# Six conditioning groups placed later in the weight stream of a two-block transformer, with the memory rows and the bias tables loading later

## The reference, cut to what matters

```python
cond = jax.nn.silu(c)
for layer in range(DEPTH):
    mod = cond @ ada_w[layer] + ada_b[layer]
    sh1, sc1, g1, sh2, sc2, g2 = jnp.split(mod, 6, axis=-1)
    h = modulate(rmsnorm(x, norm_g[layer, 0]), sh1, sc1)
    if layer % 2 == 0:
        mixed = ssd_na_mixer(h, ab_w_in[j], ...)      # h @ w_in, two branches, y @ w_out
    x = x + g1[:, None, :] * rmsnorm(mixed, norm_g[layer, 1])
    h = modulate(rmsnorm(x, norm_g[layer, 2]), sh2, sc2)
    u = jnp.square(jax.nn.relu(h @ mlp_w1[layer])) @ mlp_w2[layer]
    x = x + g2[:, None, :] * rmsnorm(u, norm_g[layer, 3])
```

## Time and profile before

| | |
|---|---|
| median of 3 runs | 1597.03 us (1594.93 to 1597.8) |
| profiled execution, its own time | 1598.08 us |
| its span | 1596.3 us |
| PE busy | 1489.3 us (93%) |
| DVE busy | 1142.4 us (72%) |
| ACT busy | 791.3 us (50%) |
| mean granted TensorE clock | 0.974 |
| 1 MB chunk issues on SyncE | 266 |

### The profile page before, as it was taken

How to read it: one execution, slowest core, us unless ns; L and a number is a source line. 1 busy time by engine, 2 the same in 40 slices (tenths; PEclk the granted TensorE clock), 3 DMA queues, 4 the chain that set the end, 5 groups by cost and what they waited for, 6 DMA issues and landing times.

```text
span 1596.3 us, 22352 instructions
## 1 busy us (share of the span) xinstructions
PE 1489.3 (93%) x8907; PEld 1276.0 (80%) x8910; DVE 1142.4 (72%) x1824; ACT 791.3 (50%) x1079; POOL 83.7 (5%) x82
## 2 busy tenths in 40 slices
PE   4779998999999999999999999889999899999998
PEld 3778875789988888877899888756786578799987
DVE  6797775599866857666786567999985675466653
ACT  4646654454533536454555435556554634354442
POOL 0000000000000000000000002940020000000000
PEclk7889999999999999999999999999999899999999
DMA  9864623369778553335566555333334243245551
GB/s 387 348 232 188 237 89 121 148 238 359 286 280 332 193 180 138 132 132 211 196 229 236 174 211 193 133 106 107 131 136 163 92 149 122 90 160 184 185 191 63
DMA packets 42518, 298.57 MB, mean 187 GB/s; under 512 B 4656, under 2 KB 4912, under 8 KB 7472
## 3 DMA queue, kind: packets, MB, share of 16 engines
q1 hardware_dynamic: 39984, 283.52, 47.9%
q0 software_dynamic: 1568, 8.39, 1.4%
q10 hardware_dynamic: 864, 5.24, 0.9%
HBM read 292.94 MB, written 4.19 MB: 186 GB/s over the span
## 4 chain that ended last, share of the span: by engine, by line
PE 46%; DVE 21%; PEld 15%; issue 8%; ACT 7%; DMA 2%; PEldq 1%; SPq 0%; ACTq 0%; DVEq 0%
PE ps L1034 19%; PE ps L1042 15%; PEld ps L1034 8%; PEld ps L1042 6%; DVE ring_at_lo L1310 6%; ACT w_hi L1299 3%; PE ps L1075 2%; DMA ring_at<-stream 2%; DVE ring_at L1171 2%; PE ps L2616 1%; DVE arena_at L2182 1%; DVE arena_at L3183 1%; PE ps L3527 1%; DVE arena_at L3192 1%; PE ps L3086 1%
## 5 line engine op out<-in xcount | busy, mean ns | idle before, releaser
L1310 DVE TENSOR_TENSOR ring_at_lo<-ring_at,w_hi 128x2048 fp32r<-128x2048 f32 (+1 forms) x218 | 496.3, 2279 | 179.4 <-ACT w_hi L1299 179.0
L1299 ACT ACTIVATE w_hi<-ring_at 128x2048 fp32r<-128x2048 f32 (+1 forms) x218 | 412.3, 1898 | 191.8 <-PE ps L1034 122.9
L1034 PE MATMUL ps<-w_hi,arena_at_lo 128*128 128x512 f32 x1104 | 305.1, 398 | 1.6 <-DVEq L4476 0.8
L1042 PE MATMUL ps<-h_hi,w_hi 128*128 128x256 f32 x1440 | 243.2, 292 | 14.8 <-DVE ring_at_lo L1310 7.8
L1034 PEld LDWEIGHTS ps<-w_hi,arena_at_lo 128*128 128x128 f32 x1104 | 204.6, 188 | 49.3 <-issue 2.7
L1042 PE MATMUL ps<-h_hi,ring_at_lo 128*128 128x256 f32 x1440 | 233.2, 284 | 0.0
L1042 PE MATMUL ps<-hT_at_lo,w_hi 128*128 128x256 f32 x1440 | 232.2, 284 | 0.0
L1042 PEld LDWEIGHTS ps<-h_hi,w_hi 128*128 128x128 f32 x1440 | 202.7, 193 | 23.0 <-issue 16.6
L1042 PEld LDWEIGHTS ps<-hT_at_lo,w_hi 128*128 128x128 f32 x1440 | 200.6, 192 | 0.0
L1042 PEld LDWEIGHTS ps<-h_hi,ring_at_lo 128*128 128x128 f32 x1440 | 199.1, 192 | 0.0
L1034 PE MATMUL ps<-ring_at_lo,arena_at_lo 128*128 128x512 f32 x552 | 172.1, 393 | 0.0
(11 more groups left out here) (464 smaller groups left out, 1662.9 us busy)
## 6 DMA issues: line engine op xcount, KB each, us to landing
ring_at<-stream SPq DMA_DIRECT2D x266, 1024.0 KB, 4.9
arena_at_lo<-kept_hi POOLq DMA_DIRECT2D x4, 1024.0 KB, 7.2
arena_at<-bias ACTq DMA_DIRECT2D x4, 768.0 KB, 8.0
kept<-arena_at POOLq DMA_DIRECT2D x4, 512.0 KB, 4.2
arena_at<-kept ACTq DMA_DIRECT2D x2, 1024.0 KB, 5.9
x_res<-x SPq DMA_DIRECT2D x1, 1024.0 KB, 10.5
arena_at<-mem POOLq DMA_DIRECT2D x1, 1024.0 KB, 12.7
kept_hi<-arena_at_lo POOLq DMA_DIRECT2D x1, 1024.0 KB, 10.5
```

Source lines behind the costliest of these rows:

```text
L1034: mm = pe.matmul(k.ps[:, bank + t, :], x_tile(f, slice(t * P, (t + 1) * P)), w, start=first and n == 0, stop=last and n == 2)
L1042: mm = pe.matmul(k.ps[:, bank + q // 2, (q % 2) * TOK:(q % 2 + 1) * TOK], w[:, q * P:(q + 1) * P], x, start=first and n == 0 and q % 2 == ...
L1299: act.activation(k.w_hi[:, s % HI, 0:n, :], k.ring[:, c % RING, 0:n, :], ACT.Identity).then_inc(k.hi_done, 1)
L1310: dve.tensor_tensor(k.w_lo[:, c % RING, 0:n, :], k.ring[:, c % RING, 0:n, :], k.w_hi[:, s % HI, 0:n, :].bitcast(F32), ALU.subtract).then_i ...
```

## The change

Three of the ten conditioning groups of `in0` go to `out0` (behind own chunks 3, 5 and 7), and the three that stay behind the first four stand behind own chunks 12, 16 and 20 instead of six groups behind 2, 5, 8, 11, 14 and 17. The order of the groups among themselves and the places from `up0` on are as before. The load of the memory rows waits on GpSimd for `chunk_used` 4, so for own chunk 3; `Inputs`, `MemRates`, `MemTurn` and `BiasLoad` are woven in later, and `SsdSteps` begins three quarters later and ends where it did. The late parameters are issued behind chunk 13 of the stream instead of chunk 10. `out0` gets `Conditions`, and two waits of TensorE on `guest_took`, in `SsdNorm` and in `Mlstm`, are gone with their arguments.

```diff
 MEM_AT = {"up0": 0, "in1": 1, "up1": 2, "in2": 3}
-GUESTS = {"in0": [-1, -1, 0, 0, 2, 5, 8, 11, 14, 17], "up0": [1, 3, 5, 7, 9, 11], "down0": [1, 4, 7, 10, 13],
+GUESTS = {"in0": [-1, -1, 0, 0, 12, 16, 20], "out0": [3, 5, 7],
+          "up0": [1, 3, 5, 7, 9, 11], "down0": [1, 4, 7, 10, 13],
           "out1": [3], "up1": [3, 9]}
@@ MemTurn.gpsimd
         pool.wait_ge(*self.norm.m["bank_turned"].at(4))
+        pool.wait_ge(k.chunk_used, self.after)
         pool.dma_start(self.rows, k.mem_dram).then_inc(k.mem_in, 16)
@@ SsdNorm.tensor
         yield
-        pe.wait_ge(k.guest_took, self.guests)
@@ all_stages
+    mem_turn.after = 4
-    out0 = PostProduct(k, "out0", src, y, junk, small)
+    out0 = PostProduct(k, "out0", src, y, junk, small, Conditions(k, mods))
-    steps_due = paced([(0, 7, 8, 36)])
+    steps_due = paced([(0, 7, 11, 36)])
-        Woven(k, in0, (Threaded(Inputs(k)), paced([(0, 1, 6, 7)])),
-              (Threaded(mem_rates), paced([(0, 2, 6, 10)])), (Threaded(mem_turn), paced([(0, 4, 6, 14)])),
-              (Threaded(tables), paced([(0, 1, 16, 17)])),
+        Woven(k, in0, (Threaded(Inputs(k)), paced([(0, 1, 10, 11)])),
+              (Threaded(mem_rates), paced([(0, 2, 17, 19)])), (Threaded(mem_turn), paced([(0, 4, 17, 25)])),
+              (Threaded(tables), paced([(0, 1, 28, 29)])),
@@ program, sync
-                if c == 10:
+                if c == 13:
```

More of the change, by code:

```diff
@@ L2223, in __init__ @@
         super().__init__(k)
-        self.first, self.guests, self.z_in = in0.first_group, k.guests, z_in
+        self.first, self.z_in = in0.first_group, z_in
         self.xc, self.zs, self.zs_r, self.xc_r, self.rows = xc, zs, zs_r, xc_r, rows
@@ L2541, with __init__ @@
 class Mlstm(Stage):
-    def __init__(self, k, qT, kT, v, o, sel, gate, h, e, sc, small, junk, hi, lo, first, guests, o_in):
+    def __init__(self, k, qT, kT, v, o, sel, gate, h, e, sc, small, junk, hi, lo, first, o_in):
         super().__init__(k)
@@ L2547, in __init__ @@
         self.h, self.e, self.sc, self.small, self.junk = h, e, sc, small, junk
-        self.hi, self.lo, self.first, self.guests, self.o_in = hi, lo, first, guests, o_in
+        self.hi, self.lo, self.first, self.o_in = hi, lo, first, o_in
         self.steps = [("cell", i) for i in range(5)] + [("norm", 0), ("cell", 5), ("turn", 0), ("cell", 6), ("turn", 1),
@@ L2824, in layer1_stages @@
     gate.follow(in1)
-    cell = Mlstm(k, qT, kT, v, o, sel, gate, h, e, sc, sm, junk, hi, lo, first, k.guests, o_in)
+    cell = Mlstm(k, qT, kT, v, o, sel, gate, h, e, sc, sm, junk, hi, lo, first, o_in)
     cell.after = mem
```

## The result

18 executions of the changed kernel have a median of 1600.48 us (1596.11 to 1604.52); 18 of the kernel before, beside them, 1595.97 (1594.03 to 1599.02). The ratio is 1.0028, its 95% interval 1.0020 to 1.0035: 4.5 us slower. The forecast was 1597.5, no difference that a measurement can tell, within 1589.5 to 1603.0. The time lies in the range. But the change costs 4.5 us where the sum had +0.5, and by the prediction's own measure (a difference of about 0.2% can be told) the kernel is slower, an outcome to which it gave 0.27. Ratios are taken over all executions, so they need not be the quotient of the two medians.

What follows compares the result with a forecast made beforehand. Before own chunk 10 of `in0` the stream, then VectorE, was taken as the bound, afterwards TensorE. Terms -4.9 + 2.4 + 1.2 + 1.8 = +0.5 us on the median 1597.03 gave 1597.5, range 1589.5 to 1603.

Steps and rivals of the forecast that it cites:

- the sum: Whole kernel: front -4.9, tables +2.4, end of `in0` +1.2, `out0` +1.8, together +0.5 us.
- The wait for the rows and its place: Front of `in0`: TensorE idle some 5 us near 60 us, VectorE some 6.5 us, waiting for the memory rows.
- VectorE's waits for ScalarE: Front, between VectorE's splits up to the last tap: 1.2, 2.7 and 0.6, together 4.5 us.
- The end of `in0`: Last guest's dots fall into the norm and the first head, a chain through VectorE: +1.2 us.
- the 7.7 of the sum: Front: the 1 MB load of memory rows, issued at 57.6, takes 7.7 us and is in at 65.3.
- The tables: Front: two table loads issued on ScalarE make VectorE stand between 0 and 4.7 us; 2.4 taken.
- the step that failed: `out0`: twelve dots mostly hidden in VectorE's idle time; one shows 1.18, the last two 0.6: +1.8 us.
- Rival 4: `out0`: half the twelve guests' dots show, 7.1 us instead of 1.8, giving 1602.8; chance 0.10.
- 1 (a long issue of the tables): Front: first table issue costs 4.7 instead of 2.4, 1599.8; in its short form 1595.1; chance 0.16 for both.
- 2 (nothing of the waits shows): Front: waits for ScalarE (4.5) and tables (2.4) are hidden; last tap at 105.5, time 1590.6; chance 0.25.
- 3 (12.7 us): Front: the memory rows' load becomes the bound, taking 12.7 us, +5.5, 1602.5; chance 0.12.
- 5 (5.4 us): Front: the memory rows land sooner, 5.4 us after the issue, -2.3, 1595.2; chance 0.07.

Runs made afterwards that it cites:

- run 6: Changed kernel with the three later groups of `in0` behind own chunks 11, 14 and 17 instead of 12, 16 and 20: 1601.66 us, ratio 1.0041 to the kernel before.
- run 3: Changed kernel with the groups of `out0` behind own chunks 1, 3 and 5 instead of 3, 5 and 7: 1598.17 us, ratio 1.0018 to the kernel before.
- run 9: The kernel before, unchanged, run once more for a second profile: 1595.03 us, 3.05 less than its first profile.
- run 2: Changed kernel with the three groups of `out0` put back into `in0` (10, 12, 14, 16, 18, 20), late loads kept: 1594.88 us, ratio 1.0002 to the kernel before.
- run 4: Kernel before with only the groups moved (`in0` 12, 16, 20; `out0` 3, 5, 7) and the `guest_took` waits removed: 1591.63 us, ratio 0.9983.
- run 11: Kernel before with groups at 10, 12, 14, 16, 18 of `in0` and one at place 3 of `out0`, nothing loading later: 1583.27 us, ratio 0.9922.
- run 12: Kernel before with groups at 10, 12, 14, 16, 18 of `in0` and one at place 5 of `out0`, nothing loading later: 1584.42 us, ratio 0.9929.
- run 1: Changed kernel with the memory rows' load no longer waiting for own chunk 3, everything else as changed: 1593.79 us, ratio 1.0000 to the kernel before.
- run 7: Kernel before with six groups at 10, 12, 14, 16, 18, 20 of `in0`, none in `out0`, nothing loading later: 1584.15 us, ratio 0.9932.

## Where the prediction held and where it failed

The time came out inside the range of 13.5 us, 3 us above the forecast. The mechanism of the front was as forecast, that of `out0` was not.

**Right.** The wait for the rows and its place: TensorE stands at the turn with VectorE and ScalarE behind it. TensorE and ScalarE of the changed kernel:

```profile
45.90 1.20 PE L1044 MATMUL ps<-h_hi,w_hi 128*128 128x256 f32 x4 [2.87 <-ACT w_hi L1301]
46.89 1.05 PE L1044 MATMUL ps<-hT_at_lo,w_hi 128*128 128x256 f32 x4
...
51.99 0.64 PE L1044 MATMUL ps<-hT_at_lo,w_hi 128*128 128x256 f32 x4
...
58.64 0.65 PE L1044 MATMUL ps<-h_hi,w_hi 128*128 128x256 f32 x4
...
67.73 1.12 PE L609 MATMUL ps<-con,arena_at 128*128 128x128 f32 x4 [4.64 <-DMA arena_at<-mem]
```

```profile
83.96 1.28 ACT L1991 ACT_TABLE_LOAD   x1
85.25 0.42 ACT L1991 ACTIVATE arena_at<-arena_at 128x256 f32<-128x256 f32 x1
...
99.57 0.88 ACTq L2305 DMA_DIRECT2D arena_at<-bias  x2
```

TensorE idles 4.64 us (forecast 5.1) and VectorE resumes behind 6.01 us of nothing (forecast 6.5). The second load of the logarithm's table is there at 83.96 us. VectorE's waits for ScalarE sum to 1.25 + 2.66 + 0.39 = 4.3 us where the sum had 4.5. From VectorE's resumption to the last tap are 42.8 us where the sum had 37.1 + 4.5 = 41.6 without the tables. The end of `in0`: TensorE's stall before the values of the first heads grew from 2.54 to 3.73 us, the 1.2 forecast, and run 6 removes it. (In both profiles the clock fell behind that stall. In run 3 it stayed at 1.00 from 205 to 230 us behind a stall of 3.71 us; set against run 9, where it did not fall either, the end of `in0` costs 1.33.)

**The time of the front.** The load was issued at 60.91 us, not 57.6. TensorE started own chunk 2 at 45.90 as forecast, but ran its first quarters at 1.2 GHz (three groups of matmuls in 2.7 us instead of 1.43), so eight quarters ended at 60.08 and not at 57.3. It had stood 2.87 us ahead of them for ScalarE, where before it stood 1.23. The load then took 6.8 us in this profile, and 7.9, 8.5 and 8.0 in runs 2, 3 and 6, issued at nearly the same time. Two of them, the changed kernel and run 3:

```profile
DMA to landing us min/median/max: 6.8/6.8/6.8
...
DMA to landing us min/median/max: 8.5/8.5/8.5
```

So the 7.7 of the sum was the right size, and the profile of the changed kernel is the quickest of the four; VectorE resumed 2.4 us late in it, and 4.4 in run 3 (72.82 us). The Trainium skill ("DMA: Bandwidth & Descriptors", section "Anatomy of one DMA — SWDGE (gpsimd) path") fits 2.0 us + bytes / 436e3, an estimate of 4.4 us for 1 MiB. The runs have 6.8 to 8.5 us and, with the load early at full stream, 12.5 to 12.9: the measurement decides.

**The tables.** The sum had 2.4 us for the first issue on ScalarE's queue, bounds 0 to 4.7. Both issues together took 0.88 us (ScalarE's rows above) and VectorE waited 0.31 behind them. In run 4, with the issue early:

```profile
62.40 4.31 ACTq L2304 DMA_DIRECT2D arena_at<-bias  x1
...
66.74 0.45 ACTq L2304 DMA_DIRECT2D arena_at<-bias  x1
```

So the length is not that of a first issue: at 62 and 68 us it is 4.31 and 5.50, at 100 us 0.45.

**The front as a whole, and some luck.** The rows came 2.4 us late, the stretch from there to the last tap took 1.2 more than 41.6, and the 2.4 for the tables were not spent: at the last tap the front is 1.2 us worse than forecast, -1.38 instead of -2.5. Yet the shift is -2.95 at the split of 194.23 us. These rows of TensorE, before and then changed, show where the rest comes from:

```profile
118.96 1.85 PE L2082 MATMUL ps<-con,arena_at 128*128 128x128 f32 x8 [2.10 <-ACT arena_at L2148]
120.45 1.20 PE L1042 MATMUL ps<-h_hi,w_hi 128*128 128x256 f32 x4
```

```profile
117.58 1.06 PE L2084 MATMUL ps<-con,arena_at 128*128 128x128 f32 x8 [1.00 <-ACT arena_at L2150]
118.40 0.72 PE L1044 MATMUL ps<-h_hi,w_hi 128*128 128x256 f32 x4
```

Own chunk 10 starts 2.05 us earlier, and its first quarter runs at 2.4 GHz behind a stall of 1.00 us, where the kernel before ran it at 1.2 GHz behind 2.10 us and lost 0.9 us (granted clock from 120 to 125 us 0.75 before, 0.66 in run 9, 1.00 changed). The sum had no such term, nor one for a ninth dot, at 114.86 us before, directly behind the last tap, which is gone too. That `out0` starts at -1.53 us, so near the -1.3 forecast, is owed to it and is luck.

**`out0`, the step that failed.** "One step, at 292.48, stands directly behind a split [...] a dot there costs 1.18. The last two come behind the post rows of group 0 [...] 0.6. +1.8 us." VectorE and then TensorE of the changed kernel:

```profile
288.74 2.28 DVE L1312 TENSOR_TENSOR ring_at_lo<-ring_at,w_hi 128x2048 fp32r<-128x2048 f32 x1
290.94 1.22 DVE L1173 CUSTOM_DVE_ANT_0 ring_at<-ring_at,arena_at 128x1024 f32<-128x1024 f32 x1
292.08 0.08 DVE L1173 DVE_READ_ACCUMULATOR2_ANT arena_at<- 128x1 f32 x1
...
318.25 1.21 DVE L1173 CUSTOM_DVE_ANT_0 ring_at<-ring_at,arena_at 128x1024 f32<-128x1024 f32 x1
319.40 0.08 DVE L1173 DVE_READ_ACCUMULATOR2_ANT arena_at<- 128x1 f32 x1
...
320.54 0.08 DVE L1173 DVE_READ_ACCUMULATOR2_ANT arena_at<- 128x1 f32 x1
```

```profile
293.04 0.63 PE L2356 MATMUL ps<-con,arena_at 128*128 128x128 f32 x4 [1.85 <-DVE arena_at L2426]
...
294.86 2.08 PE L1036 MATMUL ps<-w_hi,arena_at_lo 128*128 128x512 f32 x4
...
323.20 1.20 PE L1077 MATMUL ps<-w_hi,arena_at_lo 128*128 128x512 f32 x4 [2.49 <-DVEq L4477]
```

The dot at 290.94 costs what the step said: the shift goes from -1.53 to -0.40, 1.13 us. The sum left out what the stall does to the clock: TensorE stands 1.85 us instead of 0.71, the next four matmuls take 2.08 us, and the shift goes on to +1.13, another 1.53. And the end of the stage costs 1.41, not 0.6: both dots at 318.25 and 319.40 stand ahead of the last split, which ends 2.3 us later, and TensorE stands 2.49 instead of 1.08 us. So the term of +1.8 measured +4.08. Rival 4 had the direction, that dots show in `out0`, but neither its size (7.1 us) nor the whole mechanism: three dots of twelve show, with 2.5 us, and the clock does the rest. Runs 2 and 11, with no dot at these places, lose nothing in `out0`, and run 12, with one group at place 5, loses 2.93 us.

**The rest of the 4.5 us.** The shift in `up0` is +2.55, that at the end of the trace +1.2, the medians differ by 4.5. Three things in the traces bear on it. First, the profiled execution of before is a long one: 1598.08 us against a median of 1595.97. Run 9, at 1595.03, lacks its falls of the clock at 221 and 1370 us, and against it the changed kernel's profile is 4.25 us slower. Second, with places 3, 5 and 7 `out0` cost 4.08, 4.09, 5.11, 6.43, 6.49 and 7.01 us in six traces. Either the clock falls behind the stall at 293 us, as in the first two, or it does not; then TensorE finishes early, stands 3.6 to 4.2 us at the end of the stage and the clock falls at the start of `up0`, which costs 1.5 to 2.8. The changed kernel's profile is the cheapest of the six. Third, its rows landed soonest of four. That these make up the difference between profile and median is argued from single profiles, not shown; what is shown, by the ratios of runs 1 and 2, is that taking away either the wait for own chunk 3 or the groups of `out0` gives the whole loss back.

**The rivals.** 1 (a long issue of the tables) is out in its long form, and its short form is what happened. 2 (nothing of the waits shows) is out: 4.3 us of them do. 3 (12.7 us) is out, with 8.5 us as the longest of four loads, and 5 (5.4 us) was seen in none. That the order of things is right but the front's gain can be kept is run 4 against run 1: last tap 103.84 against 106.75; the later weaving of rows, steps and tables, with the later parameters, gives nothing back and costs 2.9 us, and the wait for chunk 3 another 6.8. The change made some 11 us of room and spent 9.7 of it in the same stretch.

## What to carry to other kernels

A load that is put behind a progress count needs its whole length, and the lateness of the count, before the first engine that waits for it; here the wait took 6.8 of 11 us. Work put into an engine's idle time is free by its place, not by the share of idle time: one dot directly in front of what TensorE waits for cost its own 1.14 us and then a clock fall of 1.5, while the four dots of a group two chunks earlier cost nothing. And one profile is one draw of the clock: compare stages between fixed marks, and have a second profile of the same kernel before explaining 2 us. A kernel with the smaller change was the better one here: with the groups out of the front and everything else left where it was, runs 7, 11 and 12 are 11 to 12 us faster than the kernel before by their ratios.

## What the runs showed of the hardware

Stalls of TensorE of 1.85 us in a well filled stage were followed by 1.2 GHz within some 2 us in four traces of eight; in the other four the clock fell behind the stall of 3.56 to 4.20 us at the stage's end. Behind stalls of 0.71, 1.08 and 1.36 us at these places it fell in none, and behind 2.49 and 2.50 us at the stage's end, in the changed kernel and run 1, neither. A stall of 2.53 us at the end of `in0` was followed by a fall in one of two profiles of the same kernel, one of 3.71 us there in run 3 by none, and the same 1.99 us at 545 us by one in both profiles of before and by none in the changed kernel. So the length of a stall alone does not say whether the clock falls. The cost of one fall was mostly 1.5 to 2.8 us, and 0.9 at 120 us. The two DMA issues on ScalarE's queue took 5.50 and 0.64 us at 68 us, 4.31 and 0.45 at 62 us in run 4, and 0.88 together at 100 us, where the DMA share is 0.51 (80 to 120 us); what makes the early ones long was not tried.
